# Head statistics of the mixed block as two short-form products of a rounded and a low part

## What is computed

```python
def rms_norm(x, g):
    return x * lax.rsqrt(jnp.mean(x * x, axis=-1, keepdims=True) + EPS) * g

def gla_branch(...):       # 4 heads, keys of 64, values of 128, chunks of 64
    ...                    # convolved q, k, v; decayed state per chunk; o = q . state
    o = rms_norm(o, g_out)             # over the 128 values of a head
    return o * silu(z)

def diff_branch(...):      # 4 heads, each with two maps of 64
    q = rms_norm(q, qn_g) * DH ** -0.5  # over 64
    k = rms_norm(k, kn_g)               # over 64
    p = softmax(masked scores)          # two maps a head
    o = (p[0] - lam * p[1]) @ v
    o = rms_norm(o, g_out) * (1 - lam_init)   # over 128
    return o * silu(z)

for l in range(2):
    h = rms_norm(x) * (1 + scale) + shift
    ...                                 # in-projection, both branches
    x = x + gate * (concat(o_gla, o_diff) @ w_out[l])
```

## Time and profile before

| | us |
|---|---|
| median of 3 runs | 1866.69 |
| lowest and highest | 1865.25 and 1867.08 |
| the profiled execution, its own time | 1865.7 |
| its span, first to last instruction | 1863.9 |
| PE busy in the span | 1803.7 |
| DVE, ACT, POOL busy in the span | 1019.5, 890.8, 881.1 |

### The profile page before, as it was taken

The page is one execution under the profiler, slowest core; times in us unless marked ns, Lnnn a source line. Parts: engine busy times, 40 slices in busy tenths (PEclk is TensorE's granted clock), DMA queues, the critical chain, the costliest instruction groups (busy, mean ns, idle before and its releaser), DMA issues.

```text
span 1863.9 us, 25940 instructions
## 1 busy us (share of the span) xinstructions
PE 1803.7 (97%) x8406; PEld 1414.2 (76%) x8406; DVE 1019.5 (55%) x1659; ACT 890.8 (48%) x1384; POOL 881.1 (47%) x1072
## 2 busy tenths in 40 slices
PE   7999979999999999999899999999999999999999
PEld 5666658888888878788778888888776777776777
DVE  5676655631563377777757513643445565636562
ACT  6676644422343356656444312433356555456562
POOL 3332336665665534343406755666543335443343
PEclk9999989999999999999999999999999999999999
DMA  4111114433443322122135423443222222222212
GB/s 169 57 57 56 57 39 151 161 124 101 152 164 101 101 78 68 60 68 68 34 106 175 148 90 124 167 138 90 79 83 66 68 68 80 80 68 68 74 63 91
DMA packets 49659, 176.82 MB, mean 95 GB/s; under 512 B 5648, under 2 KB 5776, under 8 KB 49568
## 3 DMA queue, kind: packets, MB, share of 16 engines
q1 hardware_dynamic: 42368, 149.44, 25.4%
q10 hardware_dynamic: 7200, 26.22, 4.0%
HBM read 173.54 MB, written 2.10 MB: 94 GB/s over the span
## 4 chain that ended last, share of the span: by engine, by line
PE 80%; DVE 9%; ACT 6%; issue 4%; POOL 1%; DMA 0%; DVEq 0%; ACTq 0%; SPq 0%; POOLq 0%
PE ps_g L243 16%; PE ps_g L247 16%; PE ps_g L250 16%; PE ps_zt L243 6%; PE ps_zt L247 6%; PE ps_zt L250 6%; PE ps_s L1558 1%; PE ps_zt L990 1%; ACT w_hi L215 1%; PE ps_zt L1607 1%; PE ps_o L1019 1%; PE ps_o L524 1%; PE ps_o L1622 1%; PE ps_zt L514 1%; PE ps_s L415 1%
## 5 line engine op out<-in xcount | busy, mean ns | idle before, releaser
L223 POOL TENSOR_TENSOR w_lo<-raw,w_hi 128x256 fp32r<-128x256 f32 x936 | 763.3, 846 | 815.1 <-ACT w_hi L215 813.8
L215 ACT ACTIVATE w_hi<-raw 128x1024 fp32r<-128x1024 f32 x274 | 288.8, 1054 | 375.1 <-PE ps_zt L250 246.9
L243 PE MATMUL ps_g<-h_hi,w_hi 128*128 128x512 f32 x1240 | 346.6, 409 | 9.9 <-ACT h_hi L292 8.4
L247 PE MATMUL ps_g<-h_lo,w_hi 128*128 128x512 f32 x1240 | 324.0, 391 | 1.0 <-DVE h_lo L302 1.0
L250 PE MATMUL ps_g<-h_hi,w_lo 128*128 128x512 f32 x1240 | 322.4, 390 | 0.3 <-DVE w_lo L231 0.3
L243 PEld LDWEIGHTS ps_g<-h_hi,w_hi 128*128 128x128 f32 x1240 | 224.4, 189 | 76.2 <-issue 23.6
L247 PEld LDWEIGHTS ps_g<-h_lo,w_hi 128*128 128x128 f32 x1240 | 233.3, 188 | 53.5 <-DVE h_lo L302 2.3
L250 PEld LDWEIGHTS ps_g<-h_hi,w_lo 128*128 128x128 f32 x1240 | 233.1, 188 | 50.5 <-DVE w_lo L231 0.7
L359 DVE TENSOR_TENSOR scr<-ps_zt,scr 128x512 f32<-128x512 f32 x32 | 22.2, 692 | 255.0 <-PE ps_zt L250 255.0
L846 ACT ACTIVATE scr<-ps_g 128x512 f32<-128x512 f32 x64 | 38.3, 598 | 193.1 <-PE ps_g L250 193.1
L243 PE MATMUL ps_zt<-a_hi,w_hi 128*128 128x512 f32 x512 | 128.6, 393 | 0.0
(11 more groups left out here) (211 smaller groups left out, 2396.4 us busy)
## 6 DMA issues: line engine op xcount, KB each, us to landing
raw<-weights SPq DMA_DIRECT2D x274, 512.0 KB, 3.5
scr<-ada_weights ACTq DMA_DIRECT2D x48, 512.0 KB, 4.3
x<-x_tiles SPq DMA_DIRECT2D x8, 256.0 KB, 5.0
y<-x SPq DMA_DIRECT2D x8, 256.0 KB, 3.3
scr<-csil_dram ACTq DMA_DIRECT2D x2, 512.0 KB, 5.5
lvmask<-level_masks SPq DMA_DIRECT2D x1, 960.0 KB, 9.5
mats<-squares SPq DMA_DIRECT2D x1, 448.0 KB, 6.4
vecs<-vectors SPq DMA_DIRECT2D x1, 95.5 KB, 1.9
```

The lines of the kernel that those rows point to most:

```text
L215: nc.scalar.activation(w_hi[:, t.rep % 2], raw[:, raw_slot(t)], ACT.Copy).then_inc(whi_ready, 1)
L223: ins = nc.gpsimd.tensor_tensor(w_lo[:, t.rep % 2, ks], raw[:, raw_slot(t), ks], w_hi[:, t.rep % 2, ks].bitcast(F32), ALU.subtract)
L243: nc.tensor.matmul(bank[:], w_hi[:, t.rep % 2, kk], rhs(k)[0], start=(first and n == 0), stop=False)
L247: nc.tensor.matmul(bank[:], w_hi[:, t.rep % 2, kk], rhs(k)[1], start=False, stop=False)
```

## The change

The squares of each statistic are kept in two parts of type float32r: ACT squares the source once as before and a second time with rounding into `bsq_r[:, 0]`; POOL subtracts this from the first and writes the rest, rounded, into `bsq_r[:, 1]`. The statistic is then two products with a rounded copy of the ones matrix, which ACT makes once. PE waits for the rounded squares before the first product and for the rest before the second. The new step on POOL stands in the common list at the place of the square. The other blocks' statistics stay as they are.

```diff
+        sums_r = sb("sums_r", [P, 2, P], F32R)
+        bsq_r = sb("bsq_r", [P, 2, SEQ], F32R)
...
                     n = nth(STATS, s[1:], l)
-                    pe.wait_ge(b_unit.sq_ready, n.v + 1)
+                    ones = sums_r[:, (M_HEADS, M_ONES).index(stat_src(s[1], it, l)[1])]
+                    pe.wait_ge(sums_ready, 2)
+                    pe.wait_ge(bsqhi_ready, n.v + 1)
                     if n.v:
                         pe.wait_ge(b_unit.ln_done, n.v)
-                    nc.tensor.matmul(ps_s[:], mats[:, stat_src(s[1], it, l)[1]], bsq_b, start=True,
-                                     stop=True).then_inc(b_unit.stat_ready, 1)
+                    nc.tensor.matmul(ps_s[:], ones, bsq_r[:, 0], start=True, stop=False)
+                    pe.wait_ge(bsqlo_ready, n.v + 1)
+                    nc.tensor.matmul(ps_s[:], ones, bsq_r[:, 1], start=False, stop=True).then_inc(b_unit.stat_ready, 1)
...
+        def b2_square_act(act, n, src):
+
+            b_unit.act_square(act, n, src)
+            act.activation(bsq_r[:, 0], src, ACT.Square).then_inc(bsqhi_ready, 1)
+
+        def b2_square_pool(pool, n):
+
+            pool.wait_ge(b_unit.sq_ready, n.v + 1)
+            pool.wait_ge(bsqhi_ready, n.v + 1)
+            nc.gpsimd.tensor_tensor(bsq_r[:, 1], bsq_b, bsq_r[:, 0].bitcast(F32), ALU.subtract).then_inc(bsqlo_ready, 1)
+
         def b2_act(act, l):
             T = T_B2 + l * B2_TILES
+            if l == 0:
+                for i, m in enumerate((M_HEADS, M_ONES)):
+                    act.activation(sums_r[:, i], mats[:, m], ACT.Copy).then_inc(sums_ready, 1)
...
-                        b_unit.act_square(act, nth(STATS, ("qk"[s[1]], it), l), bank)
+                        b2_square_act(act, nth(STATS, ("qk"[s[1]], it), l), bank)
...
-                        b_unit.act_square(act, n, src[:])
+                        b2_square_act(act, n, src[:])
...
+                elif (s[0] == "evac" and s[1] < 2) or s[0] == "square":
+                    name = "qk"[s[1]] if s[0] == "evac" else s[1]
+                    b2_square_pool(pool, nth(STATS, (name, s[-1]), l))
```

More of the change, by code:

```diff
@@ L1437, in build_program @@
         b_unit = Unit("b_unit", M_HEADS, DH, bsq_b, brstd_b)
+        sums_ready, bsqhi_ready, bsqlo_ready = ev("sums_ready"), ev("bsqhi_ready"), ev("bsqlo_ready")
         cv_first = ev("cv_first")
```

## The result

The changed kernel takes 1869.43 us in the median (20 runs, 1868.61 to 1871.39); the kernel before, measured beside it, 1866.55 (20 runs). The ratio is 1.0018 with a 95% interval of 1.0011 to 1.0025: slower by a little, by less than the 0.2% taken as the bound of no change, and 0.9 us above the predicted range. The profiled execution took 1869.3, with a span of 1867.4.

The account below looks back on a forecast made before the run. PE, busy 97% of the span, was taken as the bound. Terms of -4.1 + 0.8 + 0.3 + 1.6 = -1.4 us a layer, -2.8 for both, took the median from 1866.7 to 1863.9 us; range 1858.0 to 1868.5.

Parts of the forecast that it names:

- What bounds the kernel, and what leaves PE: Whole kernel: PE is busy 97% of the span; each statistic gives back 0.41 us, 32 give 13.1 if PE waits nowhere.
- the ten: q and k of heads 0, 2, 3 and four o statistics keep the whole 0.41: -4.1 us a layer.
- The subtraction's price: POOL's added subtraction per statistic: taken as 1.05 us from L1881's same shape, with 1.6 kept as the higher case.
- GLA pair 0: three statistics, a loss: Pair 0: second Square, POOL's queue and DVE contention make head 0's first transposes later: +0.8 us, in place of -1.2.
- L1801, the like operation, goes from 0.68 to 1.22 in the worst case, so I add 0.3: Pair 0: DVE's multiply L1796 is slowed by POOL working through all of it, priced at 0.3 us.
- k of head 1: Head 1: new subtraction delays the decay chain 1.4, PE waits 0.7 at v's transposes: +0.3 us net a layer.
- GLA pair 1: End of layer: half 0's subtraction stands behind two weight splits on POOL, half 1's gain is eaten: +1.6 us.
- The sum: Both layers of the stage: -4.1 + 0.8 + 0.3 + 1.6 = -1.4 us a layer, -2.8 for both.
- 0.15 to wake PE behind POOL: Where PE waits for POOL's subtraction: 0.15 us until PE goes on, used in the wait estimates.
- POOL and DVE slow each other in more places: Rival, 0.10: a subtraction adds 0.5 to DVE operations with two SBUF inputs where PE waits for DVE: 1867.3 us.
- The subtraction is the bound: Rival, 0.12: at 2.0 us on POOL, k statistics of heads 0, 2, 3 come 0.55 late: slower, 1873.6 us.

Follow-up runs that it names:

- when alone: Changed kernel with the short form only for q and k of heads 0, 2, 3 and four o statistics a layer: 1858.19 us beside 1865.66, ratio 0.9959; again 0.9957.
- Half 1 alone: Changed kernel with the short form only for half 1 of GLA pair 0, one statistic a layer: 1870.19 us, ratio 1.0019 to the kernel before.
- the run with DVE: Changed kernel with the subtraction of GLA pair 1's two statistics on DVE in place of POOL: 1863.8 us beside 1866.3, ratio 0.9983.
- the execution without a fall: Changed kernel unaltered, run again, ratio 1.0021 to the kernel before; profiled execution 1868.28 us, in which the clock didn't fall at the end of layer 0.
- POOL's two pieces: Short form only for half 1 of GLA pair 0, POOL's subtraction split into two instructions of 256 columns: 1870.86 us, ratio 1.0023 to the kernel before.

## Why the prediction was wrong

- *What bounds the kernel, and what leaves PE.* Right. 0.41 a statistic, measured 0.40 where nothing waits; the ten gave 3.9 a layer for 4.1, and as much when alone. The list of PE's waits left out the longest ones of the stage, those of the scores for the exponentials (2.1 us in all); they don't move the forecast, but they blur every comparison of single traces.
- *The subtraction's price.* The 1.05 of L1881 was too low for 1.29. L1881's second input is one column of a chunk repeated; that this is why it is faster was not tested. By itself the step did little: 0.24 on each wait for it.
- *"GLA pair 0: three statistics, a loss", +0.8; measured 1.6 and 1.5.* The chain and POOL's queue were right (PE stood 1.65 for 1.8 forecast). The step that was mis-sized is the contention: "L1801, the like operation, goes from 0.68 to 1.22 in the worst case, so I add 0.3". The multiply went from 0.91 to 1.64, so +0.73, and L1821, not counted at all, from 0.68 to 0.91. These two terms are 0.65 more, and 0.8 + 0.65 = 1.45. Half 1 alone cost 1.2, which is the second Square's 0.49 and this 0.73. The row I took as the worst case was no bound: it met a split of 256 columns, and the new subtraction is longer. The rule that the runs support was already in the rows of before: the split of the earlier trace rows ends at 1406.57 and L1796 at 1407.12, 0.55 later.
- *"k of head 1", +0.3; measured 0.37.* The chain and the number were right, the place of the wait wasn't. The decay chain came late and PE stood 0.43 (1424.36 to 1424.79) at the transposes of the attention (L1622), which by their code wait for DVE's copy behind the k multiply (it ended at 1424.69); at v's transposes, where I had 0.7, it then stood 0.04.
- *"GLA pair 1", +1.6; measured 3.4 and 3.2.* The mechanism is right, as the run with DVE shows. PE stood 2.34 for 2.0; by the distance from the first product to the next step (1544.54 to 1547.61, 3.07, for 0.86 before) half 0 costs 2.2 and not 1.65. That is +0.55, of which 0.2 is the subtraction's price. The failed step is the term that isn't there: the sum put nothing for TensorE's clock behind a wait, and the fall adds 0.9 to 1.0. The trace of before gave no row for it: PE's waits in the stage were 1.4 us at most there, and the clock was 1.00 through it. The last part is half 1: in the execution without a fall its statistic took 1.11 to the next step (1549.92 to 1551.03) for 0.86, so +0.25 where the sum had -0.05. 1.6 + 0.55 + 0.9 + 0.3 is 3.35.
- *The sum.* By what was measured, -3.9 + 1.6 + 0.4 + 3.3 = +1.4 a layer for -1.4, which is 2.8 of the stage's 3.3; the rest, some 0.5, is about the 0.6 of the scores' wait in the second layer, which the change doesn't make. The pair 1 term is the larger miss (1.7 a layer, more than half of it the clock), the contention the second (0.65). The sum also had 0.15 to wake PE behind POOL; the rows show 0.05 to 0.06 (1406.89 to 1406.94).
- *The rivals.* "POOL and DVE slow each other in more places" was the nearest in kind, at 1867.3; none had the clock. "The subtraction is the bound" is excluded: no head's k waits, though only by 0.2 us. The contention rule cited from the Trainium skill (GPSIMD Engine Reference, 1 Specifications) held. The Trainium skill's page SBUF — State Buffer, Who interferes with whom, says more: the shared port pair is an exclusive lock, and issue order decides who blocks. That the other engine is blocked for the whole instruction it states for DVE's two-port modes only, not for an operation with two SBUF inputs. The rows here show it for these too: in the traces before and after, all 28 of DVE's two-input operations on SBUF (TENSOR_TENSOR) that began inside an instruction of POOL, from 1375 on, ended 0.55 behind it, and POOL's two pieces took 1.86 when DVE came between. By the rows of before alone, the multiply would have been priced at what is left of a subtraction plus 0.55.

## What to carry to other kernels

Before a product is made cheaper by giving it a second input from a slow engine, price for each place when that engine's queue comes free, and shorten only where it is idle: ten of sixteen statistics gave 0.4%, all sixteen lost 0.2%. Where the engine's queue is full and another is idle, as DVE at the end of the layer, move the operation there. A wait of PE as long as those that brought a fall here (1.64 us and more) should be given a second price: a fall cost 0.1 where another wait stood right behind it, 0.9 to 1.0 at the end of the layer, and once 1.5 where nothing hid it.

## What was not expected of the hardware

- After waits of 1.65 and 2.34 us in an otherwise full queue, TensorE's granted clock fell to its lower level for part of the next microseconds (0.57 over 1408 to 1412, 0.69 over 1547 to 1551). It doesn't do so each time: in one execution of the changed kernel it fell behind three of the four waits, in another behind two. Over the traces of this stage it fell behind 11 of the 16 waits of 1.64 us or more, and behind none of the shorter ones (1.4 at most). What decides it was not found. With PE kept busy in the wait it fell nowhere in the stage, in two profiles.
- A DVE multiply with two inputs in SBUF and a POOL subtraction don't share but take turns: 0.69 became 1.64 behind a subtraction of 1.26 that began 0.17 earlier, and 1.10 behind one of half the columns. It kept its 0.69 when it began in the last 0.06 of a POOL instruction, and then POOL's next one was held, so that its four took 3.42 for 2.83.
